# A one-core hybrid layer and a two-layer GLU/attention stack in fp32: another order of the mixer's steps, a fourth buffer for the split weights, and most weight differences moved from GpSimd to VectorE

## The chip, the core and the metric

One NeuronCore of a Trainium2 chip runs the whole program; the other cores are idle. The metric is device time in microseconds of one execution, as the median of several. In a profile PE is TensorE's matmul, PEld its weight load, DVE VectorE, ACT ScalarE, POOL GpSimd and SP the engine whose queue issues the weight loads. An "L" and a number is a line of the kernel.

## What is computed

Input is one sequence of 256 tokens with 1024 features. A first block (state-space scan, a top-k attention, an attention to a memory, a mixture of 32 experts) is followed by two layers of this form:

```python
for l in range(2):
    h = rmsnorm(x, ffn1_norm[l])
    x = x + 0.5 * swiglu(h, ffn1_w_gate[l], ffn1_w_up[l], ffn1_w_down[l])   # 1024 -> 2816 -> 1024
    h = rmsnorm(x, mix_norm[l])
    q_a, k_a, v_a, q_b, k_b, v_b, r_b, g_lr, gate_a, gate_b = split_cols(h @ w_in[l], IN_SPLITS_2)
    o_a = swa_attention(q_a, k_a, v_a, q_gain, k_gain, sinks, cos, sin)     # 8 heads of 64, window 128
    log_a = log_sigmoid(g_lr @ gla_w_gate[l] + gla_gate_bias[l]) / 16
    o_b = gla_attention(q_b, k_b, v_b, log_a)                              # 4 heads, chunks of 64
    o_b = rmsnorm(o_b, gla_out_norm[l]) * silu(r_b)
    merged = sigmoid(gate_a) * (o_a @ w_proj_a[l]) + sigmoid(gate_b) * (o_b @ w_proj_b[l])
    x = x + merged @ w_out[l]
    h = rmsnorm(x, ffn2_norm[l])
    x = x + 0.5 * swiglu(h, ffn2_w_gate[l], ffn2_w_up[l], ffn2_w_down[l])
```

All of it is fp32. The part between the two GLUs is called the mixer here.

## The kernel before, in words

**Units.** A weight matrix comes as units of 128 partitions x 2048 values (1 MB): four 128-row blocks of 512 columns (a `panel` of 1024 rows is two units, `kh` 0 and 1). In the two layers each unit goes through four stations: SP loads it into one of three buffers `raw`; ScalarE copies it, rounded, into one of three `w_hi` (`hi`, L1682); an engine subtracts, `w_lo = raw - w_hi`, into one of three `w_lo`; TensorE takes three products for each block, hi x hi, lo x hi and hi x lo (`split_products`, L969 to L971), 24 matmuls a unit. SP may load unit n once the difference of unit n-3 is made (semaphore `lo_split`), ScalarE may round unit n once TensorE is done with unit n-3 (`unit_used`). In the GLUs the differences are VectorE's (`lo`, L2177). In the mixer the first two (`qa`) are VectorE's and the other 34 of a layer (`mid[2:]`) are GpSimd's (L3185), which has nothing else to do there.

**The order of the work** is written out by hand on each engine; nothing is scheduled. Between its own steps ScalarE rounds the next units by a helper `ahead`, one or two beyond the step at hand. TensorE takes in a mixer, in this order: panels `qa`, `kva`, `qb`, `kb`, the turned heads (`sqT`, `skT`), `glr`, the decay product `lgT` (L1582), then for each half t of the tokens the scores (L1114), panel `vb` c=t, the turning of the probabilities (L1128) and their product with the values (L1253); then panels `rb` 0 and 1 and `ga` 0, the turned keys `gkT`, `A` (L1604), `kv` (L1615), panels `ga` 1 and `gb` 0, the GLA output `ob` (L1629, L1633), panel `gb` 1, `pa`, the turned rows `o`, `pb`, `wo2` with the turned rows `m2` and `n3` between, and then the GLU `ff2`.

**What the others do meanwhile.** VectorE: squares and norm of the heads, rotation (L2395 to L2412), the score's mask and maximum (L2504 to L2515), the normalising (L2519 to L2523), the decay chain that goes back and forth with ScalarE (L3060 to L3086: a running sum L3065 within chunks, exponents on ScalarE between), the GLA state (L3104), the output rows (L3119), the split of turned activations (`a_lo`, L2195, L2210), the weighting by the gates (L3135 to L3140). ScalarE: `hi`, copies out of PSUM (L1689), the softmax's exponents (L1831), the exponents of the decays, roots and the three gates; `rb` is copied raw and goes through Silu after both panels.

**The scan of the first block.** For 16 tiles T TensorE computes an input `bu` (`drive`, L1198), VectorE rotates and scans it (L2351 to L2364), GpSimd rotates back (L3193 to L3201, two buffers `s_out`), TensorE reads out (`read_out`, L1188, L1190). A `drive` needs one of four PSUM banks. To fill the time TensorE also takes 20 pieces of panels (L1057), one a tile up to T=11 and two a tile from T=12. Before tiles 1, 5 and 9 VectorE computes angles of 8.5 us for ScalarE's sine tables.

**The GLU loops** run four trips of six units as hardware loops on TensorE, ScalarE, VectorE and SP, and then a tail.

Of the kernel before, what the change touches and what calls it, by code (L numbers as in the profile page):

```python
# [47 lines left out]
SPLIT = 3  # L48
# [5 lines left out]
SCAN_PIECES = [(n, kh, t) for n in SCAN_PANELS for kh in range(2) for t in range(2)]  # L54
IN2 = dict(qa=(0, 512), kva=(512, 256), qb=(768, 512), kb=(1280, 512), vb=(1792, 1024),
# [63 lines left out]
def plan():  # L119
# [263 lines left out]
    mark("gates", "rb", "ga", "gb")  # L383
# [6 lines left out]
    small_bank[0] = 0  # L390
    small(("rrow", "n2"))
    for t in range(2):
        small(("sqT", t))
    small(("skT", 0))
    panel("qb")
    fill(("qbT", 0), 4); fill(("qbT", 1), 5)
    panel("kb")
    fill(("kbT", 0), 6); fill(("kbT", 1), 7)
# [4 lines left out]
    for i, n in enumerate(("vb", "rb", "ga", "gb")):
        for c in range(2):
            panel((n, c))
            for t in range(2):
                if (n, c) != ("gb", 1):
                    fill((n, c, t), 4 + 2 * (c % 2) + t)
    attention("swa", 4)
# [7 lines left out]
    for t in range(2):  # L417
        for hp in range(2):
            fill(("ob", t, hp), 4 + 2 * t + hp)
    fill(("gb", 1, 0), 6); fill(("gb", 1, 1), 7)  # L420
# [20 lines left out]
    assert RAW == SPLIT == 3 and all(n % RAW == 0 for n in units.per.values()), units.per  # L441
# [4 lines left out]
def bass_hybrid_moe_then_swa_gla(nc, A, out):  # L446
# [4 lines left out]
    with ExitStack() as ctx:  # L451
# [14 lines left out]
        at_hi, w_hi = placed("w_hi", [P, SPLIT, UNIT], F32R)  # L466
        at_lo, w_lo = placed("w_lo", [P, SPLIT, UNIT], F32R)
        raw_r = view_at("raw_r", [P, RAW, UNIT], at_raw, F32R)
        lo_f = view_at("lo_f", [P, SPLIT, UNIT], at_lo, F32)
# [50 lines left out]
        def area(off, *shape):  # L520
# [7 lines left out]
            if len(shape) == 4:  # L528
# [62 lines left out]
                   + [(lo_f[:, i, :], w_lo[:, i, :]) for i in range(SPLIT)])  # L591
# [3 lines left out]
        moe_hi = [y_flat[1][:, 1024:1024 + UNIT]] + [w_hi[:, (PRE_UNITS + i) % SPLIT, :] for i in (2, 0, 1)]  # L595
# [52 lines left out]
        gab = area(o, 2, 2, 1024); o += 4096  # L648
# [15 lines left out]
        hid2 = area(o + 3072, 2, 512)  # L664

# [31 lines left out]
        class Engine:  # L697
# [159 lines left out]
        def _(sp):  # L857
# [3 lines left out]
            def load(name):  # L861

                if E.regs:
                    sp.wait_ge(lo_split, E.unit_value(name) - (RAW - 1))
                sp.dma_start(E.view(raw, name), unit_source(name, E.regs)).then_inc(weights_loaded[E.slot(name)], 16)

            def load_loop(tag):
                with sp.Fori(0, trips_of(tag)) as i:
# [80 lines left out]
        def _(pe):  # L949
# [13 lines left out]
            def unit(name):  # L963

                pe.wait_ge(lo_split, E.unit_value(name) + 1)
                return E.view(w_hi, name), E.view(w_lo, name)
# [234 lines left out]

            for T in range(3):
                drive(T)
            for T in range(SSM_TILES):
                if T + 3 < SSM_TILES:
                    drive(T + 3)
                for piece in SCAN_PIECES[T + max(0, T - 12):T + 1 + max(0, T - 11)]:
                    scan_piece(*piece)
                if T >= 2:
                    read_out(T - 2)  # L1210
            read_out(SSM_TILES - 2)
# [99 lines left out]
            def down_unit(k, c, slot, acc, meanwhile=None):  # L1311
                hi, lo = unit(("d", k, c))
                for t in range(2):
                    for j in range(unit_shape[("d", k, c)][0]):
                        at = (slice(None), slot, j, slice(t * P, t * P + P))
                        m = split_products(acc[t][c], y_hi[at], y_lo[at], hi[:, j, :], lo[:, j, :], False, False,
# [5 lines left out]
            def glu_finish(tag, acc, src, w, following):  # L1322
# [11 lines left out]
                down_unit(k, 0, 0, acc, turn_end)  # L1334
                pe.wait_ge(done["hidden_turned"], nth("hidden_turned", (*z, 1)))
                down_unit(z, 0, 1, acc)
                for t in range(2):
                    close((tag, "acc", 0, t), acc[t][0])
                down_unit(k, 1, 0, acc, following)
                down_unit(z, 1, 1, acc)  # L1340
# [1961 lines left out]
```

## Time and profile before

| | before |
|---|---|
| median of 3 runs | 2443.76 us (2443.68 to 2447.91) |
| profiled execution | 2445.01 us, its span 2443.2 us |
| granted TensorE clock, mean | 0.969 |
| busy: PE / DVE / ACT / POOL | 2290.7 / 1500.2 / 1156.2 / 403.9 us |
| chain that ended last | PE 72%, DVE 15%, ACT 6%, issue 4%, POOL 2% |
| HBM read | 494.45 MB, 203 GB/s over the span |

The span is the time from the first to the last instruction of the profiled execution; 1.8 us of that execution's time lie outside it. Stages by time: first block without experts 0 to 412 us, experts to 1100, then layer 0 with its mixer from 1292.8 to 1589.4, and layer 1 with its mixer from 1962.4 to 2257.6. The mean clock is that of TensorE as granted, 1.00 for 2.4 GHz; the lower level is 1.2 GHz.

### The profile page before, as it was taken

Reading aid. Unit: us, or ns where it says so; the run is one execution under the profiler, and the core shown is the slowest. Engines: PE = TensorE matmul, PEld = TensorE weight load, DVE = VectorE, ACT = ScalarE, POOL = GpSimd, SP = SyncE. Lnnn points to the kernel's source line nnn. Section 1 sums busy time; section 2 is a strip of 40 time slices with the busy share of each in tenths; the row PEclk is TensorE's granted clock in tenths of the full one; section 3 lists DMA queues with packets and bytes.
Section 4 is the critical chain, followed back from the end, with each engine's and each line's share of the span. In section 5 each row is a group of like instructions: output and inputs, shape, how many; then the busy total and the mean of one; then the engine's idle time right before and its main releaser. Section 6 shows DMA issues by size and latency. Waiting matters only on the chain.

```text
span 2443.2 us, 27659 instructions
## 1 busy us (share of the span) xinstructions
PE 2290.7 (94%) x9901; PEld 1637.4 (67%) x9901; DVE 1500.2 (61%) x1497; ACT 1156.2 (47%) x1174; POOL 403.9 (17%) x147
## 2 busy tenths in 40 slices
PE   6899995999999999999999888999999998899999
PEld 4345544566565656548888766788888887667887
DVE  6967337888888887875556442555554573435554
ACT  4122413676767666645334545443343345464432
POOL 2640000000000000000005355600000043555000
PEclk8899997999999999999999889999999999999999
DMA  6234242899999999974545243455455452434553
GB/s 218 69 104 137 87 159 96 329 367 356 373 357 369 358 370 360 368 308 161 183 155 166 78 138 106 154 189 189 163 197 179 156 165 73 134 121 155 189 189 104
DMA packets 166435, 496.64 MB, mean 203 GB/s; under 512 B 10272, under 2 KB 21792, under 8 KB 136400
## 3 DMA queue, kind: packets, MB, share of 16 engines
q1 hardware_dynamic: 164528, 491.70, 57.0%
q10 hardware_dynamic: 1616, 3.24, 0.4%
q8 instruction: 53, 0.87, 0.1%
q0 software_dynamic: 208, 0.59, 0.1%
q14 instruction: 30, 0.25, 0.0%
HBM read 494.45 MB, written 1.05 MB: 203 GB/s over the span
## 4 chain that ended last, share of the span: by engine, by line
PE 72%; DVE 15%; ACT 6%; issue 4%; POOL 2%; DMA 0%; DVEq 0%; ACTq 0%; POOLq 0%
PE ps L969 12%; PE ps L970 12%; PE ps L971 12%; PE ps L1401 9%; PE ps L1037 6%; PE ps L1382 5%; PE ps L1386 5%; PE ps L1128 2%; POOL w_lo L3185 2%; PE ps L1057 2%; PE ps L1370 1%; ACT w_hi L1682 1%; PE ps L1439 1%; PE ps L1253 1%; PE ps L1114 1%
## 5 line engine op out<-in xcount | busy, mean ns | idle before, releaser
L1682 ACT ACTIVATE w_hi<-raw 128x2048 fp32r<-128x2048 f32 x204 | 379.4, 1866 | 423.5 <-PE ps L971 388.7
L3185 POOL TENSOR_TENSOR w_lo<-raw,w_hi 128x2048 fp32r<-128x2048 f32 x68 | 314.6, 4645 | 1558.2 <-ACT w_hi L1682 1558.2
L969 PE MATMUL ps<-w_hi,a_hi 128*128 128x512 f32 (+1 forms) x1216 | 476.0, 391 | 34.2 <-POOL w_lo L3185 23.8
L970 PE MATMUL ps<-w_lo,a_hi 128*128 128x512 f32 (+1 forms) x1216 | 466.3, 383 | 0.0
L971 PE MATMUL ps<-w_hi,a_lo 128*128 128x512 f32 (+1 forms) x1216 | 465.1, 382 | 0.0
L2177 DVE TENSOR_TENSOR w_lo<-raw,w_hi 128x2048 fp32r<-128x2048 f32 (+1 forms) x136 | 303.0, 2229 | 249.0 <-ACT w_hi L1682 243.4
L969 PEld LDWEIGHTS ps<-w_hi,a_hi 128*128 128x128 f32 x1216 | 234.6, 193 | 81.6 <-issue 26.6
L971 PEld LDWEIGHTS ps<-w_hi,a_lo 128*128 128x128 f32 x1216 | 234.2, 193 | 44.5
L970 PEld LDWEIGHTS ps<-w_lo,a_hi 128*128 128x128 f32 x1216 | 234.7, 193 | 40.5
L1382 PE MATMUL ps<-w_hi,W_r 128*128 128x512 f32 x468 | 190.8, 408 | 5.4 <-DVE w_lo L2839 4.7
L969 PE MATMUL ps<-w_hi,y_hi 128*128 128x512 f32 x384 | 153.8, 401 | 0.0
L970 PE MATMUL ps<-w_lo,y_hi 128*128 128x512 f32 x384 | 150.3, 391 | 0.0
L971 PE MATMUL ps<-w_hi,y_lo 128*128 128x512 f32 x384 | 149.8, 390 | 0.0
L1382 PEld LDWEIGHTS ps<-w_hi,W_r 128*128 128x128 f32 x468 | 89.3, 191 | 55.1 <-issue 30.9
L2839 DVE TENSOR_TENSOR w_lo<-lo_f,w_hi 128x2048 fp32r<-128x2048 f32 x48 | 109.2, 2290 | 19.7 <-ACT w_hi L1880 15.8
L1910 ACT ACTIVATE xn<-ps 64x512 f32<-64x512 f32 x78 | 46.4, 595 | 140.8 <-PE ps L1386 139.9
L2839 DVE TENSOR_TENSOR raw_r<-raw,w_hi 128x2048 fp32r<-128x2048 f32 x40 | 90.8, 2290 | 22.5 <-ACT w_hi L1880 20.5
L1401 PE MATMUL ps<-lo_f,W 128*64 128x512 f32 x232 | 103.2, 594 | 0.0
L1401 PE MATMUL ps<-raw,W 128*64 128x512 f32 x216 | 96.5, 596 | 0.0
L1386 PE MATMUL ps<-raw_r,W_r 128*128 128x512 f32 x240 | 95.1, 396 | 0.0
L1386 PE MATMUL ps<-w_lo,W_r 128*128 128x512 f32 x232 | 92.7, 400 | 0.0
L1880 ACT ACTIVATE w_hi<-lo_f 128x2048 fp32r<-128x2048 f32 x48 | 90.4, 1901 | 3.9 <-ACT W_r L1926 2.1
(412 smaller groups left out, 3664.6 us busy)
## 6 DMA issues: line engine op xcount, KB each, us to landing
raw<-in_w_in SPq DMA_DIRECT2D x56, 1024.0 KB, 5.1
raw<-in_ffn_w_gate SPq DMA_DIRECT2D x44, 1024.0 KB, 5.1
raw<-in_ffn_w_up SPq DMA_DIRECT2D x44, 1024.0 KB, 5.1
raw<-in_ffn_w_down SPq DMA_DIRECT2D x40, 1024.0 KB, 5.0
raw<-in_w_up SPq DMA_DIRECT2D x30, 1024.0 KB, 7.9
raw<-in_w_gate SPq DMA_DIRECT2D x30, 1024.0 KB, 7.1
lo_f<-in_w_up SPq DMA_DIRECT2D x30, 1024.0 KB, 8.4
lo_f<-in_w_down SPq DMA_DIRECT2D x29, 1024.0 KB, 7.6
```

The costliest lines, as they stand in the source:

```text
L969: pe.matmul(dst, a_h, b_h, start=first, stop=False, **kw)
L970: pe.matmul(dst, a_h, b_l, start=False, stop=False, **kw)
L971: return pe.matmul(dst, a_l, b_h, start=False, stop=final, **kw)
L1037: m = pe.matmul(dst[t][:, 0:w], lhs[:, k0 + k, t * P:t * P + P], b[:, k, :], start=i == k == 0, stop=i == last and k == nk - 1 and t == 0, ...
L1382: m = pe.matmul(dst, a, hi[:, k * 512:k * 512 + 512], start=half == 0 and k == 0, stop=False, skip_group_check=True)
L1386: m = pe.matmul(dst, a, lo[:, k * 512:k * 512 + 512], start=False, stop=half == 1 and k == 3, skip_group_check=True)
L1401: m = pe.matmul(dst[c], hidT[:, 2 * half + r, :], w[:, r * D + c * 512:r * D + c * 512 + 512], start=half == 0 and r == 0, stop=half == 1 ...
L1682: act.activation(E.view(w_hi, name), E.view(raw, name), ACT.Copy).then_inc(hi_split, 1)
L1880: act.activation(E.expert_hi(u), E.expert_raw(u)[0], ACT.Copy).then_inc(expert_hi, 1)
L2177: tt(E.view(w_lo, name), E.view(raw, name), E.view(w_hi, name).bitcast(F32), ALU.subtract)\
L2839: tt(E.expert_raw(u)[1], E.expert_raw(u)[0], E.expert_hi(u).bitcast(F32), ALU.subtract).then_inc(expert_lo, 1)
L3185: pool.tensor_tensor(E.view(w_lo, name), E.view(raw, name), E.view(w_hi, name).bitcast(F32), ALU.subtract)\
```

## The change

- **Buffers.** Four `hi` and four `lo` buffers (`SPLIT = 4`); the fourth pair lies in the back of `y_hi` and `y_lo`. `raw` stays at three. The end rows of the GLU's hidden values, which lay there, go to a part of W.
- **Differences.** In a mixer VectorE makes 30 of the 36 (28 more than before), GpSimd six: the two of `gb` 1 and the four of `rb`.
- **Order.** `ga` and `gb` come before `rb`; the two units of a panel are steps of their own on TensorE (`wide(n, c, kh)`), with the attention's steps put between units. Scores of both halves come early, and the second half's probabilities lie in the area of the gates, so that they don't wait for the first half's. `rb` leaves PSUM through Silu, the single large Silu is gone. `o` is turned half by half between `pa` and `pb`.
- **Scan.** Four of the pieces go to the tiles before which VectorE computes angles (two after T=1, one after T=5 and T=9); from T=12 there is one a tile. ScalarE copies the panels' results out before it computes tables 2 and 3.
- **Loops.** The GLU loops of the two layers are written out, on all four engines.

```diff
-SPLIT = 3
+SPLIT = 4
+PIECES_WAITING = {1: 2, 5: 1, 9: 1}
...
+        hi_bufs, lo_bufs = ([w[:, i, :] for i in range(RAW)] + [y[:, 1024:1024 + UNIT]]
+                            for w, y in ((w_hi, y_flat[0]), (w_lo, y_flat[1])))
...
-                with pe.Fori(0, trips_of(tag)) as i:
+                for i in range(trips_of(tag)):
...
+            pieces = list(SCAN_PIECES)
             for T in range(SSM_TILES):
                 if T + 3 < SSM_TILES:
                     drive(T + 3)
-                for piece in SCAN_PIECES[T + max(0, T - 12):T + 1 + max(0, T - 11)]:
-                    scan_piece(*piece)
+                scan_piece(*pieces.pop(0))
                 if T >= 2:
                     read_out(T - 2)
+                for _ in range(PIECES_WAITING.get(T, 0)):
+                    scan_piece(*pieces.pop(0))
...
+                scores(0)
+                wide("vb", 0, 0)
...
+                wide("vb", 0, 1)
+                scores(1)
+                wide("vb", 1, 0)
+                turn_probs(0)
+                wide("vb", 1, 1)
                 pe.wait_ge(done["values"], nth("values", "swa"))
...
+                attended(0)
+                wide("ga", 0, 0)
+                turn_probs(1)
+                wide("ga", 0, 1)
+                attended(1)
+                wide("ga", 1, 0)
+                wide("ga", 1, 1)
+                wide("gb", 0, 0)
+                wide("gb", 0, 1)
                 pe.wait_ge(done["decayed"], nth("decayed", "ku"))
...
-                pool.wait_ge(lo_split, E.unit_value(("kva", 0)))
-                for name in mid[2:]:
-                    lo(name)
+                pool.wait_ge(lo_split, E.unit_value((("gb", 1), 0)))
+                for name in straight((("gb", 1), 0), (("rb", 1), 1)):
+                    pool.wait_ge(hi_split, E.unit_value(name) + 1)
+                    pool.tensor_tensor(E.lo_view(name), E.raw_view(name), E.hi_view(name).bitcast(F32), ALU.subtract)\
+                        .then_inc(lo_split, 1)
```

The two tables of order below show where the terms of the prediction lie.

TensorE at the start of the scan, before and then with the change. The matmuls into `m_full` are pieces (four for each), those from `W` 128x256 are drives, those from `s_out` read-outs.

```order
L1057 MATMUL ps<-lo_f,m_full 128x512 x4
L1198 MATMUL ps<-W 128x256 x2
L1057 MATMUL ps<-lo_f,m_full 128x512 x4
L1198 MATMUL ps<-W 128x256 x2
L1057 MATMUL ps<-lo_f,m_full 128x512 x4
L1188 MATMUL ps<-s_out,W 32x256
```

```order
L1080 MATMUL ps<-lo_f,m_full 128x512 x4
L1221 MATMUL ps<-W 128x256 x2
L1080 MATMUL ps<-lo_f,m_full 128x512 x12
L998 MATMUL ps<-zero_b 1x1
L1221 MATMUL ps<-W 128x256 x2
L1080 MATMUL ps<-lo_f,m_full 128x512 x4
```

Two further pieces stand ahead of the third drive.

VectorE in the decay chain of a mixer, before and then with the change. `w_lo<-raw,w_hi` and `y_lo<-raw,y_hi` of 128x2048 are differences of units; the CAST and the difference behind it take the second half of the attention's output out of PSUM.

```order
L3060 SCALAR_TENSOR_TENSOR W<-W,xn 128x1024
L3062 TENSOR_SCALAR W<-W 128x1024
L3065 SCALAR_TENSOR_TENSOR xn<-W 128x256 x4
L3069 TENSOR_TENSOR W<-xn 128x1024
L3072 TENSOR_TENSOR xn<-W 128x1024
L3076 SCALAR_TENSOR_TENSOR W<-W 128x1024
L3078 TENSOR_TENSOR W<-xn 128x1024
L3081 SCALAR_TENSOR_TENSOR W<-W 128x1024
```

```order
L3205 SCALAR_TENSOR_TENSOR W<-W,xn 128x1024
L3207 TENSOR_SCALAR W<-W 128x1024
L3210 SCALAR_TENSOR_TENSOR xn<-W 128x256 x4
L3214 TENSOR_TENSOR W<-xn 128x1024
L2267 TENSOR_TENSOR w_lo<-raw,w_hi 128x2048
L2273 CAST y_hi<-ps 128x4x128
L2275 TENSOR_TENSOR y_lo<-ps,y_hi 128x4x128
L3219 TENSOR_TENSOR xn<-W 128x1024
L3223 SCALAR_TENSOR_TENSOR W<-W 128x1024
L3225 TENSOR_TENSOR W<-xn 128x1024
L2267 TENSOR_TENSOR w_lo<-raw,w_hi 128x2048
L3229 SCALAR_TENSOR_TENSOR W<-W 128x1024
```

A difference now stands in VectorE's queue after each return to ScalarE, and the chain starts before the attention's output is out.

## Rows read from the trace of the kernel before

**Rows 1.** The page: the span in 40 equal slices, PE busy and granted clock, in tenths.

```profile
PE   6899995999999999999999888999999998899999
...
PEclk8899997999999999999999889999999999999999
```

**Rows 2.** Busy time by stretch: two mixers, scan, two GLU stretches; columns in the first line.

```profile
core 0: us, PE busy (x) PEld busy (x) DVE busy (x) ACT busy (x) POOL busy (x), PEclk, DMA share, GB/s
...
1292.80:1589.40 296.60, 263.65 (x1308) 213.85 (x1306) 140.10 (x132) 148.32 (x180) 157.90 (x34) 0.94 0.38 126
1962.40:2257.60 295.20, 262.30 (x1309) 212.57 (x1308) 140.32 (x132) 148.32 (x180) 156.69 (x34) 0.94 0.38 127
...
1110.00:1290.00 180.00, 180.00 (x874) 148.41 (x873) 96.25 (x70) 71.44 (x50) 0.00 (x0) 1.00 0.55 181
```

**Rows 3.** Waits of PE in the first mixer (us in total, times, longest), four of ten.

```profile
PE ps L969 <- POOL w_lo L3185: 12.2, 6, 3.8
PE ps L1128 <- DVE W L3140: 4.3, 1, 4.3
PE ps L969 <- DVE a_lo L2195: 3.9, 2, 3.6
PE ps L1098 <- POOL w_lo L3185: 2.5, 1, 2.5
```

**Rows 4.** Chain of the first mixer's decays, a stretch of it: start, us, what.

```profile
1429.05 1.93 ACT w_hi L1682
1431.05 4.97 POOL w_lo L3185
```

**Rows 5.** The same unit of 24 matmuls at two clocks: stretches with their busy times.

```profile
1425.50:1432.70 7.20, 7.12 (x25) 5.52 (x25) 4.78 (x4) 4.04 (x3) 1.68 (x2) 0.78 0.44 146
1468.20:1474.00 5.80, 5.72 (x25) 4.38 (x24) 0.00 (x0) 4.41 (x3) 2.96 (x1) 1.00 0.00 0
```

**Rows 6.** Timeline of DVE, two places of the first mixer: start, us.

```profile
1319.19 1.23 DVE L2395 TENSOR_TENSOR W<-W,C 128x1024 f32<-128x1024 f32 x1 [3.32 <-ACT C L1698]
1320.45 5.54 DVE L2398 TENSOR_TENSOR W<-W,C 128x1024 f32<-128x1024 f32 x1
...
1549.67 0.69 DVE L3138 TENSOR_TENSOR W<-ps,W 128x512 f32<-128x512 f32 x1
1550.40 4.16 DVE L3140 TENSOR_TENSOR W<-W 128x512 f32<-128x512 f32 x1
```

**Rows 7.** DVE's groups in the first mixer: busy us, mean ns, idle before.

```profile
L3140 DVE TENSOR_TENSOR W<-W 128x512 f32<-128x512 f32 x4 | 15.2, 3812 | 0.1
L2195 DVE TENSOR_TENSOR a_lo<-W,a_hi 128x512 fp32r<-128x512 f32 x10 | 13.3, 1328 | 1.2 <-ACT a_hi L1720 0.3
```

**Rows 8.** The difference on DVE (page) and POOL's (its tile, ns min/median/max).

```profile
L2177 DVE TENSOR_TENSOR w_lo<-raw,w_hi 128x2048 fp32r<-128x2048 f32 (+1 forms) x136 | 303.0, 2229 | 249.0 <-ACT w_hi L1682 243.4
...
L3185 POOL TENSOR_TENSOR w_lo<-raw,w_hi x34: 1447/4606/5672, 1300.7 to 1575.7; 128x2048 fp32r<-128x2048 f32 x33, 128x128 fp32r<-128x128 f32 x1
```

**Rows 9.** The page: loads of units, count, KB each, us from issue to landing.

```profile
raw<-in_w_in SPq DMA_DIRECT2D x56, 1024.0 KB, 5.1
```

**Rows 10.** The scan: PE's waits, then the last rows of DVE and POOL.

```profile
PE ps L1198 <- DVE xn L2353: 18.9, 3, 8.7
...
152.65 1.57 DVE L2364 TENSOR_TENSOR_SCAN W<-W,xn 128x256 f32<-128x256 f32 x1
...
158.74 1.30 POOL L3193 TENSOR_TENSOR xn<-W 128x512 f32<-128x512 f32 x1
160.12 1.26 POOL L3195 TENSOR_TENSOR W<-W 128x512 f32<-128x512 f32 x1
165.19 0.73 POOL L3199 TENSOR_TENSOR s_out<-W,xn 128x256 f32<-128x256 f32 x1 [3.81 <-PE ps L1190]
166.00 0.73 POOL L3201 TENSOR_TENSOR s_out<-W,xn 128x256 f32<-128x256 f32 x1
```

**Rows 11.** Waits of DVE in the first mixer: us in total, times, longest.

```profile
DVE C L2519 <- ACT xn L1831: 10.8, 2, 5.4
```

More of the change, by code:

```diff
@@ L382, in plan @@
     mark("evacuated", *(("ob", t, hp) for t in range(2) for hp in range(2)))
-    mark("gates", "rb", "ga", "gb")
+    mark("evacuated", *(("rb", c, t) for c in range(2) for t in range(2)))
+    mark("gates", "ga", "gb")
+    for t in range(2):
+        mark("maxed", ("swa", t)); mark("exped", ("swa", t)); mark("probs", ("swa", t))
+        mark("probs_turned", *(("swa", t, p) for p in range(4)))
+        mark("branch", ("swa", t))
     panel("qa")
@@ L394, in plan @@
     small(("skT", 0))
[L395 to L398, printed above, removed]
     unit(("glr", 0), 8, 16)
     small(("glrT", 0))
+    for p in range(4):
+        small(("swa", "S", 0, p))
     for i in range(2):
         small(("lgT", i))
[L403 to L409, printed above, removed]
+    for n, c in ((n, c) for n in ("vb", "ga", "gb", "rb") for c in range(2)):
+        panel((n, c))
+        for t in range(2):
+            fill((n, c, t), 4 + 2 * c + t)
+    for p in range(4):
+        small(("swa", "S", 1, p))
+    for t in range(2):
+        for p in range(4):
+            small(("swa", "PT", t, p))
+        small(("swa", "O", t))
     for t in range(2):
@@ L418, in plan @@
         for hp in range(2):
[L419 to L420 removed]
+            small(("ob", t, hp))
     mark("rstd", "o")
@@ L439, in plan @@
     end(LAYERS)
-    assert RAW == SPLIT == 3 and all(n % RAW == 0 for n in units.per.values()), units.per
+    assert RAW == 3 and all(n % RAW == 0 for n in units.per.values()), units.per
     assert tiles.per["moe"] % MOE_RAW == 0 and tiles.n == 6 * TILES
@@ L1539, in glu @@
                 acc = zeroed_sums(tag)
-                with pe.Fori(0, trips_of(tag)) as i:
+                for i in range(trips_of(tag)):
                     regs[tag] = i
@@ L1721, in turned_hi @@
                         act.wait_ge(done["turned_hi"], nth("turned_hi", (tag, hh, t)))
-            def ahead(name, extra=1):
-                split_ahead(E, stretch, hi, name, extra)
             act.wait_ge(const_loaded, 16)
@@ L2001, in glu @@
                 silu((tag, "first"), dst, 512, None, r)
-                with act.Fori(0, trips_of(tag)) as i:
+                for i in range(trips_of(tag)):
                     regs[tag] = i
@@ L2176, in lo @@
                 dve.wait_ge(hi_split, E.unit_value(name) + 1 + ahead)
[L2177 removed]
+                tt(E.lo_view(name, ahead), E.raw_view(name, ahead), E.hi_view(name, ahead).bitcast(F32), ALU.subtract)\
                     .then_inc(lo_split, 1)
[L2180 to L2181 removed]
             def split_out(src, hi_, lo_):
@@ L2958, in glu @@
                 dve.wait_ge(done["rstd"], nth("rstd", root))
-                with dve.Fori(0, trips_of(tag)) as i:
+                for i in range(trips_of(tag)):
                     regs[tag] = i
-                    step.begin(i, steps)
                     lo(("g", L, 0))
```

380 lines of the change are left out of this document (253 added, 127 removed).

## The prediction

> **What bounds the kernel now.** The page's rows by slices of 61 us come first [rows 1]: TensorE is under 90% busy in eight slices of 40, and the five of them behind the first block (numbers 22 to 24 and 33 and 34, from 0) lie in the two mixers, 1292.8 to 1589.4 us and 1962.4 to 2257.6; in the first of them the clock is down too. The table of busy time by stretch [rows 2] says how much is there. In the first mixer TensorE is busy 263.65 of 296.60 us at a clock of 0.94, in the second 262.30 of 295.20 at 0.94; in a GLU stretch of 180 us it is busy 180.00 at 1.00, so that there is nothing to win in the GLUs. Idle are 32.95 and 32.90 us. What the clock costs is read from one pair [rows 5]: the same unit of 24 matmuls takes 7.2 us after a wait of TensorE and 5.8 us in a stretch without one. A clock of 0.94 over a mixer is at most 0.06 x 296.6 = 17.8 us, and 17.7; a part of it lies in the waits themselves and costs nothing more, so I take 15.5 each, that is eleven units at 1.4. TensorE's own work in a mixer is then 263.6 - 15.5 = 248 us.
>
> Who holds it up is in the waits [rows 3]: the differences of GpSimd 12.2 + 2.5, VectorE behind three other steps. The chain [rows 4] shows why a unit comes late: ScalarE rounds it (1.93), and only then GpSimd takes 4.97, all of it seen by TensorE, because the rounding stood behind the chain of decays.
>
> The timeline of VectorE [rows 6] shows a second cost of GpSimd's work. Two operations of 128x1024 follow each other, the first takes 1.23 us and the second 5.54; a 128x512 that reads PSUM takes 0.69 and the next, with both inputs in SBUF, 4.16. In groups [rows 7]: L3140 has 15.2 us for four where 0.69 each would be 2.8, and L2195 has 13.3 for ten where it would be 6.9. That is 12.4 + 6.4; with the same subtraction for the other lines of this kind I count some 45 us of 140.1 in a mixer in which VectorE stood behind GpSimd.
>
> **The change part by part.**
>
> *28 differences from GpSimd to VectorE.* The difference takes 2.23 us in the mean there, with its smaller forms, and 4.6 us on GpSimd [rows 8]. A full one is 2.29, so VectorE gets 28 x 2.29 = 64 us and loses the 45 us of blocking, but for what the last six units leave of it: 140 + 64 - 45 = 159 us of 248, or 64%. ScalarE stays at 148.3 [rows 2]. Neither is full; TensorE is the bound if the units are ready in time.
>
> *Are they?* I laid the three queues beside each other by the durations of these rows, from the first `qa` unit on as time 0. TensorE takes a unit in about 5.6 us; a load lands in 5.1 [rows 9] and rounding takes 1.9 [rows 4]. With four buffers ScalarE may round three units ahead. The narrow places are these, as the time at which the thing is ready and the time at which TensorE wants it: the turned heads' source 39 and 42 (10 us of VectorE after the roots, where the blocked ones take 23 now); probabilities of the first half 67 and 71; the turned probabilities 75 and 78; `ga` 0 78 and 82; decays `k` 116 and 122; GLA state 140 and 144; output rows 170 and 177; `m2` first half 200 and 201; `m2` second half 211 and 210.6; its `a_lo` 214 and 213. All the other units are ready 7 us or more ahead. So nine places are met with 1 to 7 us to spare and the last two are not. I leave 8 us for each mixer: 5.5 of idle time, which is the two late ones and half of what nine places with a mean slack of 4 us can miss, and 2.5 for two units at the lower clock. The bounds are 0 (all are met) and 24 (each of ten places misses by 1 us and pays 1.4 us for a slow unit behind it). **Term: -(48.4 - 8) = -40.4 us for each mixer, -80.8 for both**, between -65 and -97.
>
> *The six that stay with GpSimd.* They are rounded from about 108 to 142 and wanted from 124 to 166, one each 5.6 us or slower because of `kv` and `ob` between. At 4.6 us each they keep up, by 11 us or more. VectorE has then only the last decays (one or two blocked, 3 to 4 us each, with 6 us to spare) and operations that read PSUM. The trace says what the other direction costs: among GpSimd's 34 differences beside a busy VectorE the longest is 5.67 against a median of 4.61 [rows 8], so 1.1 us more at most. The Trainium skill (SBUF — State Buffer, Who interferes with whom) says that a VectorE instruction with two SBUF inputs and a GpSimd one that reads SBUF exclude each other for the whole instruction, whichever came first. By it each of the six could stand 2.3 us behind a difference on VectorE, 14 us in all and not 6.6; the slack of 11 us at the first unit would not be used up at once, so the sum would be the same, but the third rival gets more weight from it. VectorE's part of the rule the trace bears out [rows 6].
>
> *Order of the softmax, Silu by panels, `o` by halves.* The work is the same. Their gain is inside the term above: the waits for VectorE's L2523, L3055, L2187 and for `a_lo` [rows 3] go under units.
>
> *Scan.* TensorE waits three times for a bank, 18.9 us together [rows 10]; four pieces of some 3.6 us, 14.4 us, go there and are missing behind T=12. What that is worth is set by the others: VectorE's last scan ends at 152.65 + 1.57 = 154.2, and nothing TensorE does differently makes it earlier by more than 0.7. GpSimd turns that tile only after a wait of 3.81 us for TensorE's read-out, and is done at 166.7; unhindered its four steps of 1.30, 1.26, 0.73 and 0.73 with gaps end at 154.2 + 4.3 = 158.5. **Term: -8.2 us**, between 0 (ScalarE's later tables hold up the copies out of PSUM, and the pieces with them) and -14.4. Behind the scan TensorE is busy with gates, so this is kept.
>
> *Loops written out.* TensorE is busy 180.00 of 180.00 us over a loop with its trips [rows 2]; a trip's end costs nothing that could be saved. Zero, with all queues of TensorE's six units a trip as cover. The Trainium skill (Runtime: NRT & Kernel Launch, Instruction fetch mechanics) states that a taken branch out of the loaded window forces a fetch, and that kernels prefer unrolling. By it the loops' ends would give something back; no row shows it.
>
> *Buffers, end rows.* No instruction more. The fourth pair is free in the GLUs because the end rows moved. Zero.
>
> **Sum.** 2445.0 - 80.8 - 8.2 = 2356.0 for the profiled execution. That one stands 1.25 us above the median of the runs, 2443.8, so I say **2354.8 us**, 3.6% faster. A measurement of this kernel tells 0.2%, 4.9 us, from no change.
>
> **Rivals.**
>
> 1. *Half of the mixers' loss stays.* VectorE's queue is in order, and its differences now stand behind its own waits for ScalarE; a unit that misses makes `raw` free later, then load, rounding and difference (5.1 + 1.9 + 2.3 = 9.3 us) follow, of which only 5.6 lie under the unit before. For it: the narrow places above. Against it: `raw` of the next units is loaded well ahead in my three queues. It gives 2445 - 48.4 - 8.2 = 2388, median 2387.
>
> 2. *Slower: VectorE's waits become TensorE's.* VectorE waits in a mixer some ten times for ScalarE or for a bank between two differences; the softmax's wait is 5.4 us now [rows 11]. If each reached TensorE in full, with a slow unit behind it, that is 10 x (5.4 + 1.4) = 68 us in a mixer against 48.4 today: 2 x 19.6 - 8.2 = 31 us slower, 2476. It decides from (96.8 + 8.2) / 20 - 1.4 = 3.9 us a place. Against it: three units are rounded and split ahead, 17 us of TensorE's work.
>
> 3. *GpSimd's six hold up `rb`.* With `rb` now last, a late difference there is followed by `pa`, whose difference VectorE makes only after GpSimd's last. Six times (2.3 + 1.4) less the slack of 11: 11 us in a mixer, 2377.
>
> 4. *The change does not do what it says*, because the mixers wait for the weights: then TensorE's idle time stays as it is and only the scan is gained, 2437. Against it: the DMA engines have a share of 0.38 in a mixer, and 0.55 in the GLUs, where TensorE never waits [rows 2].
>
> **How the numbers follow.** My forecast 0.75, rival 1 0.12, rival 3 0.06, rival 4 0.02, rival 2 0.03, and 0.02 for no change by several small things. The forecast's own range is 2445 - 97 - 14.4 = 2334, less 1.25 = 2332, to 2445 - 65 - 0 = 2380; its ends meet only if all terms go one way, so I take 2338. At the top the range goes to 2382, which takes in rival 3. Faster by over 0.2%: 0.75 + 0.12 + 0.06 + 0.02 = 0.95; within: 0.02; slower: 0.03.
>
> **What would show it.** Mixers of 256 us (first `qa` unit to the GLU) with TensorE idle under 8 us and a clock of 0.98 or more in each; all slices from 1100 us on at 9 in both rows of the page; the rotation's and the gates' operations on VectorE (now L2398, L3140) at 1.2 and 0.7 us; VectorE busy some 160 us in a mixer and GpSimd some 28; the last read-out of the scan at 159 to 160 us. The forecast is wrong if TensorE's waits for a difference come back under VectorE's name with more than 8 us, if VectorE is over 80% busy in a mixer, if TensorE's units in a mixer stay at 7.2 us, or if a GLU stretch is below full.

## The result, and the profile after

| | before | after |
| --- | --- | --- |
| time, median | 2443.72 us | **2349.31 us** (2348.77 to 2350.29, 4 runs) |
| ratio of after to before | | 0.9612, 95% interval 0.9595 to 0.9629 |
| profiled execution: its time, its span | 2445.0, 2443.2 us | 2350.29, 2348.2 us |
| mixer 1, first `qa` unit to the GLU | 296.6 us | 251.0 us |
| mixer 2 | 295.2 us | 247.7 us |
| last read-out of the scan | 167.8 us | 160.0 us |

The change makes the kernel 3.9% faster; the prediction was 2354.8 us in a range of 2338 to 2382. The page of the changed kernel, its slices and its counters; it answers to [rows 1]:

```profile
PE 2260.8 (96%) x9901; PEld 1615.0 (69%) x9901; DVE 1536.2 (65%) x1553; ACT 1150.2 (49%) x1172; POOL 144.8 (6%) x91
...
PE   7889996999999999999999999999999999999998
...
PEclk9989997999999999999999999999999999999999
```

From the eighth slice on every digit of both rows is a 9, but for the last of the upper row, where five of these were below it in the upper row before. What the mixers hold now, in the busy time by stretch (columns in the first line; mixer 1, mixer 2, a GLU stretch), answers to [rows 2]:

```profile
core 0: us, PE busy (x) PEld busy (x) DVE busy (x) ACT busy (x) POOL busy (x), PEclk, DMA share, GB/s
1290.30:1541.30 251.00, 248.12 (x1309) 202.77 (x1308) 158.29 (x160) 146.65 (x179) 27.48 (x6) 0.99 0.44 149
1914.70:2162.40 247.70, 244.87 (x1307) 200.64 (x1306) 158.25 (x160) 146.59 (x179) 27.49 (x6) 1.00 0.45 151
1100.00:1280.00 180.00, 180.00 (x873) 148.53 (x872) 96.77 (x70) 74.63 (x55) 0.00 (x0) 1.00 0.51 170
```

TensorE is idle 2.9 us in each mixer where it was 32.9. All but 0.1 us of it stands in two rows of its waits in mixer 1 (us in total, times, longest), and mixer 2 has the same two; the ten of before [rows 3] are gone:

```profile
PE ps L1137 <- DVE W L3149: 2.3, 1, 2.3
PE ps L1121 <- issue: 0.5, 1, 0.5
```

VectorE is blocked at one place only. Its timeline at the rotation, which had 1.23 and 5.54 us [rows 6], and its groups in mixer 1, where the gates' weighting (now L3292) had 3812 ns and `a_lo` (now L2283) 1328 ns [rows 7]:

```profile
1319.19 1.22 DVE L2483 TENSOR_TENSOR W<-W,C 128x1024 f32<-128x1024 f32 x1
1320.44 1.23 DVE L2486 TENSOR_TENSOR W<-W,C 128x1024 f32<-128x1024 f32 x1
```

```profile
L2283 DVE TENSOR_TENSOR a_lo<-W,a_hi 128x512 fp32r<-128x512 f32 x10 | 6.9, 692 | 0.8
L3231 DVE TENSOR_TENSOR W<-xn 128x1024 f32<-128x1024 f32 x1 | 5.5, 5507 | 0.0
...
L3292 DVE TENSOR_TENSOR W<-W 128x512 f32<-128x512 f32 x4 | 2.8, 693 | 0.1
```

That place is one operation of the decays, L3231, which one of GpSimd's six units holds up: 5.5 us where its neighbours of the same size take 1.2. The six themselves (GpSimd's line, both mixers, ns min/median/max) show no slowing; before, the longest took 5672 ns [rows 8]:

```profile
L3375 POOL TENSOR_TENSOR w_lo<-raw,w_hi x9: 4552/4583/4674, 1415.6 to 2059.7; 128x2048 fp32r<-128x2048 f32 x9
L3375 POOL TENSOR_TENSOR y_lo<-raw,y_hi x3: 4604/4608/4662, 1405.3 to 2041.3; 128x2048 fp32r<-128x2048 f32 x3
```

The scan is another matter. PE's timeline at its end answers to [rows 10]:

```profile
153.19 0.62 PE L1211 MATMUL ps<-s_out,W 128*32 128x256 f32 x2 [1.67 <-POOL s_out L3360]
...
158.09 1.06 PE L1211 MATMUL ps<-s_out,W 128*32 128x256 f32 x2 [3.85 <-POOL s_out L3360]
158.94 1.06 PE L1213 MATMUL ps<-s_out,W 128*32 128x256 f32 x2
159.79 0.24 PE L998 MATMUL ps<-zero_b 128*1 128x1 bf16 x2
159.96 16.03 PE L1060 MATMUL ps<-raw,a_full 128*128 128x512 f32 x32
...
183.24 14.00 PE L1060 MATMUL ps<-lo_f,a_full 128*128 128x512 f32 x32
```

The last read-out ends at 160.0, 7.8 us earlier than the 167.8 of before. But TensorE has nothing left to do while it waits 1.67 and 3.85 us for GpSimd, and what follows runs slower: a read-out 1.06 us and not 0.62, the first gate 16.03 us where the next, of equal size, takes 14.00. The same work behind the scan, from the start of that first gate to the same scores, in the kernel before and in the changed one, by stretch (columns as above):

```profile
167.80:287.20 119.40, 115.13 (x412) 63.77 (x409) 66.99 (x124) 42.28 (x79) 0.00 (x0) 1.00 0.36 117
```

```profile
159.96:284.46 124.50, 120.22 (x411) 66.04 (x408) 67.00 (x124) 42.31 (x79) 0.00 (x0) 0.96 0.33 110
```

At a clock of 1.00 it took 119.4 us, at 0.96 it takes 124.5. In this one execution only 7.8 - 5.1 = 2.7 us of the scan's gain are left at the end of that stretch. So two questions stand: is that give-back a property of the change, and which part of the change earned the mixers' 93 us?

### The profile page after: what moved, and what is told of

Read it like the earlier page. It is cut to its first block, busy times and chain, and to the rows that moved or that the text cites. A ratio compares the mean times of both kernels' runs of the same rounds, so it can differ in the third digit from the quotient of the medians.

```text
span 2348.2 us, 26777 instructions
## 1 busy us (share of the span) xinstructions
PE 2260.8 (96%) x9901; PEld 1615.0 (69%) x9901; DVE 1536.2 (65%) x1553; ACT 1150.2 (49%) x1172; POOL 144.8 (6%) x91
## 4 chain that ended last, share of the span: by engine, by line
PE 81%; DVE 12%; issue 4%; ACT 3%; POOL 0%; DMA 0%; DVEq 0%; ACTq 0%; POOLq 0%
PE ps L992 15%; PE ps L993 14%; PE ps L994 14%; PE ps L1428 9%; PE ps L1060 7%; PE ps L1409 5%; PE ps L1413 5%; PE ps L1151 3%; PE ps L1397 2%; PE ps L1466 1%; PE ps L1137 1%; DVE W_r L2927 1%; DVE xn L2445 1%; ACT w_hi L1935 1%; DVE W L2450 1%
## 5 line engine op out<-in xcount | busy, mean ns | idle before, releaser
L2267 DVE TENSOR_TENSOR w_lo<-raw,w_hi 128x2048 fp32r<-128x2048 f32 (+2 forms) x144 | 315.6, 2204 | 126.5 <-ACT w_hi L1737 119.9
L1737 ACT ACTIVATE w_hi<-raw 128x2048 fp32r<-128x2048 f32 (+2 forms) x153 | 281.3, 1848 | 212.1 <-PE ps L994 178.3
L992 PE MATMUL ps<-w_hi,a_hi 128*128 128x512 f32 (+1 forms) x904 | 347.8, 385 | 0.0
L993 PE MATMUL ps<-w_lo,a_hi 128*128 128x512 f32 (+1 forms) x904 | 341.5, 378 | 0.0
L994 PE MATMUL ps<-w_hi,a_lo 128*128 128x512 f32 (+1 forms) x904 | 341.1, 377 | 0.0
L2267 DVE TENSOR_TENSOR y_lo<-raw,y_hi 128x2048 fp32r<-128x2048 f32 x48 | 110.0, 2293 | 50.0 <-ACT y_hi L1737 47.6
L1737 ACT ACTIVATE y_hi<-raw 128x2048 fp32r<-128x2048 f32 x51 | 97.8, 1917 | 59.9 <-PE ps L994 50.3
L992 PE MATMUL ps<-y_hi,a_hi 128*128 128x512 f32 (+1 forms) x312 | 120.1, 385 | 1.3 <-DVE a_lo L2283 1.3
L993 PE MATMUL ps<-y_lo,a_hi 128*128 128x512 f32 (+1 forms) x312 | 116.8, 375 | 0.0
L994 PE MATMUL ps<-y_hi,a_lo 128*128 128x512 f32 (+1 forms) x312 | 116.6, 374 | 0.0
```

The source lines that it names most:

```text
L992: pe.matmul(dst, a_h, b_h, start=first, stop=False, **kw)
L993: pe.matmul(dst, a_h, b_l, start=False, stop=False, **kw)
L994: return pe.matmul(dst, a_l, b_h, start=False, stop=final, **kw)
L1737: act.activation(E.hi_view(name, ahead), E.raw_view(name, ahead), ACT.Copy).then_inc(hi_split, 1)
L2267: tt(E.lo_view(name, ahead), E.raw_view(name, ahead), E.hi_view(name, ahead).bitcast(F32), ALU.subtract)\
```

## The experiments

Each time is a median beside runs of the kernel before on the same chip. The kernel before took 2445.5 to 2447.7 us on the four chips, so it is the ratios that compare across rows; each is uncertain by 0.001 to 0.002, which is 2 to 4 us:

| kernel | us | ratio to before (95%) |
| --- | --- | --- |
| changed kernel, once more (`c_after`) | 2348.9 | 0.9603 (0.9590 to 0.9616) |
| GpSimd makes the mixers' differences (`m1_pool`) | 2377.5 | 0.9713 (0.9698 to 0.9728) |
| two units rounded ahead, not three (`m3_three`) | 2396.4 | 0.9805 (0.9789 to 0.9821) |
| both of these (`m5_pool_three`) | 2399.2 | 0.9799 (0.9783 to 0.9815) |
| the six units on VectorE too (`m2_nosix`) | 2348.1 | 0.9597 (0.9584 to 0.9610) |
| scan as before (`s1_oldscan`) | 2355.0 | 0.9620 (0.9607 to 0.9633) |
| before with the new scan alone (`s3_scan_only`) | 2437.9 | 0.9969 (0.9958 to 0.9980) |
| one piece of the scan held back (`s2_hold`) | 2347.3 | 0.9599 (0.9586 to 0.9612) |
| before with loops written out (`l1_written_out`) | 2446.0 | 0.9996 (0.9987 to 1.0005) |
| low rank first on VectorE (`m4_glr`) | 2339.5 | 0.9566 (0.9553 to 0.9579) |
| three waits taken away (`b2`) | 2336.2 | 0.9550 (0.9537 to 0.9563) |
| the same, six on VectorE (`b3`) | 2335.9 | 0.9543 (0.9530 to 0.9556) |

### Engine, buffer or order?

The changed kernel with the mixers' differences back on GpSimd, everything else kept:

```diff
 def lo(name, ahead=0):
+    if name in mid[2:]:
+        return
...
-pool.wait_ge(lo_split, E.unit_value((("gb", 1), 0)))
-for name in straight((("gb", 1), 0), (("rb", 1), 1)):
+pool.wait_ge(lo_split, E.unit_value(mid[2]))
+for name in mid[2:]:
```

> The changed kernel, but in both mixers GpSimd takes all differences from the third unit on, as in the kernel before; order, fourth buffer pair, scan and written-out loops stay as changed. It tells who earned the mixers' 45.6 and 47.3 us: the engine, or the order and the buffer. Theory A (the prediction's): the engine. VectorE is again held up by GpSimd (rotation's second operation of 128x1024 5.5 us and not 1.23), and a late unit takes 4.6 us of GpSimd where VectorE takes 2.3: mixers of 280 to 297 us against 251 and 248, time 2410 to 2445. Theory B: the order and the three units ahead cover GpSimd's 4.6 us, which lie under a unit's 5.7 us of TensorE: mixers of 250 to 265 us, time 2350 to 2380, though VectorE's operations are as slow as in A.

2377.5 us: theory B. Mixer 1 by stretch, and the longest of TensorE's waits in it:

```profile
1290.00:1552.60 262.60, 248.83 (x1305) 202.12 (x1304) 155.20 (x132) 146.37 (x179) 158.00 (x34) 0.98 0.44 142
```

```profile
PE ps L1151 <- DVE W L2502: 4.6, 1, 4.6
...
PE ps L992 <- POOL y_lo L3377: 0.5, 1, 0.5
```

VectorE's own work is 158.3 less 29 differences of 2.29, some 92 us, so 63 us of its 155.2 are blocking, more than before. (The 92 us hold the 4.3 us by which L3231 was held up, and the 155.2 hold 4.6 us for the two differences that stay with VectorE; the two nearly cancel.) Yet the mixer takes 263 us and not 297 (the second one 265), and hardly a unit is late any more (0.5 us for a GpSimd difference where it was 14.7 [rows 3]). What TensorE waits for are VectorE's own steps: the rotation comes 4.6 us late. Most of the mixers' gain does not need the new engine.

Next, the buffer. All four pairs stay in place, and ScalarE waits as if there were three:

```diff
-act.wait_ge(unit_used, E.unit_value(name) + (ahead - (SPLIT - 1)))
+act.wait_ge(unit_used, E.unit_value(name) + (ahead - (RAW - 1)))
```

> The changed kernel, but ScalarE rounds only two units ahead as in the kernel before, so that the fourth pair of buffers holds nothing that TensorE is not working on. Theory A (the fourth pair carries the order: the units' slack of 7 us or more shrinks by one unit of 5.6 us): TensorE waits for differences behind the chains of ScalarE, 3 to 8 us in each mixer, 2356 to 2370 us. Theory B (the fourth pair does little, VectorE's 2.3 us a unit is quick enough): 2349 to 2353.

2396.4 us: neither. The direction is A's, the size more than twice what A allows. The edit reaches the GLUs' rounding too, but there TensorE stays busy for 300.00 of 300.00 us; the loss lies in the mixers, 276.6 and 272.0 us. By stretch, then the largest waits of TensorE in mixer 1, and ScalarE's timeline ahead of the 6.1 us one:

```profile
1286.40:1563.00 276.60, 257.33 (x1306) 209.51 (x1305) 158.66 (x160) 145.57 (x179) 27.35 (x6) 0.94 0.41 135
1600.00:1900.00 300.00, 300.00 (x1415) 245.78 (x1414) 163.16 (x117) 119.93 (x85) 0.00 (x0) 1.00 0.55 182
```

```profile
PE ps L992 <- ACT W L1744: 6.1, 1, 6.1
PE ps L1151 <- DVE W L3292: 4.2, 3, 2.6
PE ps L1676 <- ACTq L1747: 3.3, 1, 3.3
PE ps L1137 <- DVE W L3149: 3.3, 1, 3.3
```

```profile
1463.59 1.92 ACT L1737 ACTIVATE w_hi<-raw 128x2048 fp32r<-128x2048 f32 x1 [13.55 <-PE ps L994]
1465.41 1.29 ACT L1744 ACTIVATE xn<-ps 128x512 f32<-128x512 f32 x2
...
1475.77 0.21 ACT L1753 ACTIVATE C<-C 128x8 f32<-128x8 f32 x1
...
1479.23 1.49 ACT L1744 ACTIVATE W<-ps,C 128x512 f32<-128x512 f32 x2
```

This is a mechanism that I had under none of my terms. ScalarE's queue is in order, and the rounding of `pa` 0 stands ahead of the copies of `ob`, the output's statistics and the copies of `rb`. With three pairs it may round only when TensorE has let go of a unit, and waits 13.55 us for that. Behind it the copies and statistics start at 1465 and end at 1476; the copies of `rb`, at 1479, are what TensorE then waits 6.1 us for. With the fourth pair the same rounding waits 3.01 us, and the copies of `ob` start 154 us into the mixer and not 179:

```profile
1441.54 1.91 ACT L1737 ACTIVATE w_hi<-raw 128x2048 fp32r<-128x2048 f32 x1 [3.01 <-PE ps L994]
1443.85 0.60 ACT L1744 ACTIVATE xn<-ps 128x512 f32<-128x512 f32 x1 [0.40 <-PE ps L998]
```

No wait of TensorE in that mixer is for a unit; the work behind the rounding comes late. The fourth pair buys ScalarE's queue its freedom, not the units their slack.

Both parts undone together:

> The changed kernel with both of its parts for the mixers undone together, and only their order kept: GpSimd takes the differences from the third unit on, and ScalarE rounds two units ahead. Each undone alone gave 2377.5 us (engine) and 2396.4 us (buffer) against 2348.9. Theory A (the two losses are of the same kind, a unit that is late, and add up or more): 28.5 + 47.5 = 76 us, 2425 us, or above it. Theory B (they cover one another: while TensorE waits for the rounding, GpSimd's 4.6 us are hidden): 2397 to 2410. Against 2440, the kernel before with the new scan alone (2446.4 - 6.1), it tells what the order alone is worth: 15 us or less by A, 30 to 43 by B.

2399.2 us: theory B. The largest waits of TensorE in mixer 1 are those of the buffer's run, with one for VectorE's copies behind the rotation (L3120) added:

```profile
PE ps L1151 <- DVE W L3120: 7.0, 1, 7.0
PE ps L992 <- ACT W L1744: 6.1, 1, 6.1
PE ps L1676 <- ACTq L1747: 3.3, 1, 3.3
```

One more level was needed, the kernel before with the scan's two edits alone (`PIECES_WAITING`, and `tables` behind `vm` and `kvi`):

> The kernel before with nothing but the new order of the scan's pieces and tables. It gives the level from which the order, the buffer and the engine in the mixers start. Theory A (the scan's gain is independent of the mixers): 6.1 us as in the changed kernel (2355.0 against 2348.9), 2440 to 2442 where the kernel before takes 2446.5 to 2447.5. Theory B (in the kernel before, TensorE's clock falls behind the shorter scan too, at 155 and at 200 us, and takes it back): 2444 to 2447. In the profile the last read-out at 160 us in both.

2437.9 us, a ratio of 0.9969: theory A, if anything a little more. With these the change divides, as the difference of the ratios times 2446 us; each of these prices is uncertain by some 3 to 5 us:

| step | from, to | worth |
| --- | --- | --- |
| scan | 1, 0.9969 | 7.6 us |
| order in the mixers, with loops and end rows | 0.9969, 0.9799 | 41.6 us |
| fourth pair, GpSimd still subtracting | 0.9799, 0.9713 | 21.0 us |
| VectorE subtracts | 0.9713, 0.9603 | 26.9 us |

The last two may be taken the other way round, and then they read differently: with three pairs the engine is worth nothing (0.9799 against 0.9805), and the pair on top of it 49 us. Neither figure alone is "the" value of its part; together they are worth 48 us. The 41.6 us are those of all moves of the order together; no run parts them, so which of them earned it (scores early, gates ahead of `rb`, Silu by panels, `o` by halves) stays open.

### Were the six needed on GpSimd?

```diff
-for name in straight((("gb", 1), 0), (("rb", 1), 1)):
-    pool.wait_ge(hi_split, E.unit_value(name) + 1)
-    pool.tensor_tensor(...)
...
 dve.wait_ge(done["decay"], nth("decay", 2))
+lo((("gb", 1), 0))
...
```

and the other five on VectorE behind the decays, the masks and the states.

> The changed kernel with the six units between decays and the output's statistics on VectorE too; GpSimd makes no difference in the mixers. Theory A (VectorE has room: 10.4 and 17.8 us of waiting in that very stretch): VectorE gets 6 x 2.3 = 14 us more in a mixer and TensorE sees none of it, 2347 to 2351 us against 2349.3. Theory B (the split was needed: VectorE's steps of the decays and of the state come late by up to 14 us): 5 us or more in each mixer, 2359 or more. Theory C (GpSimd's six did hold VectorE up): VectorE's operations on the decays shorten and the time falls by over 2 us.

2348.1 against 2348.9 us: theory A. Mixer 1 by stretch, and the decay operation that was blocked:

```profile
1284.90:1535.90 251.00, 248.13 (x1307) 202.94 (x1308) 167.46 (x166) 146.91 (x179) 0.00 (x0) 0.99 0.44 149
```

```profile
L3235 DVE TENSOR_TENSOR W<-W x2: 1219/1219/1219, 1403.5 to 2027.9; 128x1024 f32<-128x1024 f32 x2
```

VectorE gets 13.7 us of differences and gives back 4.3 at that operation: 167.5 for 158.3. TensorE's waits are the same two. The six cost TensorE nothing on GpSimd, and nothing on VectorE.

### Does the scan's gain last?

First the scan of the kernel before in the changed one, with ScalarE's tables at their old places too:

```diff
-scan_piece(*pieces.pop(0))
-if T >= 2:
-    read_out(T - 2)
-for _ in range(PIECES_WAITING.get(T, 0)):
-    scan_piece(*pieces.pop(0))
+for _ in range(1 + (T >= 12)):
+    scan_piece(*pieces.pop(0))
+if T >= 2:
+    read_out(T - 2)
```

> The changed kernel with the scan of the kernel before: one piece at a time and two from T = 12 on, tables before the first three copies. Theory A (most of the scan's gain is given back through TensorE's clock): the last read-out is at 167 to 168 us and not at 160.0, the gate behind it takes 14.0 us and not 16.03, and the time is 2351 to 2354 (2349.3 + 2.7). Theory B (the scan's 8 us are kept to the end, and the difference of 2.7 us at 258 us has another cause): 2356 to 2359.

2355.0 us, 6.1 above the changed kernel, between the two (by the ratios, 0.9620 against 0.9603, it is 4.2 us, give or take 4.5). Its profile says what A says (read-out at 167.8, gate at 14.00 us, no low clock behind), the median nearly what B says. The changed kernel once more explains it:

> The changed kernel unaltered, once more, on the chip of this call: the value that the other kernels of the call are to be held against, and two more mixers and one more scan in a profile. If a fall of TensorE's clock behind a wait is a matter of the single execution and not of the program, this profile shows it in other places than the first one did: behind the scan (at 155 and at 200 us in the first) and behind the 2.33 us wait for the turned heads (mixer 1 yes, mixer 2 no in the first). Time 2347 to 2351 us.

2348.9 us. The clock behind the scan and in the mixers, 10 and 15 us from the end of the scan (155), the first scores (200) and the heads' scores of each mixer, in its profile:

```profile
1335.00:1350.00 15.00, 14.22 (x50) 10.91 (x51) 10.63 (x12) 2.20 (x4) 0.00 (x0) 0.77 0.55 175
1960.00:1975.00 15.00, 14.84 (x53) 11.32 (x54) 10.16 (x11) 2.10 (x5) 0.00 (x0) 0.77 0.59 195
155.00:165.00 10.00, 7.32 (x15) 3.26 (x16) 4.78 (x8) 2.55 (x3) 2.47 (x3) 0.66 0.07 28
200.00:210.00 10.00, 9.94 (x32) 5.45 (x33) 7.19 (x21) 2.39 (x4) 0.00 (x0) 1.00 0.07 28
```

and in the first profile of the same kernel:

```profile
155.00:165.00 10.00, 6.91 (x13) 3.02 (x14) 4.41 (x7) 2.54 (x3) 2.80 (x4) 0.66 0.00 0
200.00:210.00 10.00, 8.99 (x23) 5.28 (x24) 6.53 (x20) 3.18 (x6) 0.00 (x0) 0.66 0.17 67
1335.00:1350.00 15.00, 12.67 (x57) 9.69 (x55) 14.33 (x16) 4.44 (x4) 0.00 (x0) 0.77 0.54 179
1960.00:1975.00 15.00, 12.67 (x67) 9.81 (x65) 13.88 (x14) 5.00 (x6) 0.00 (x0) 1.00 0.49 162
```

So in one kernel the clock falls behind the same wait in one execution and not in the other: at 200 us only in the first, in mixer 2 only in the second. The clock is at 1.2 instead of 2.4 GHz for some 6.8 us (a mean of 0.66 over 10 us is 6.8 us at half speed, one of 0.77 over 15 is 6.9), which costs 3.3 us in a mixer: mixer 2 took 247.7 us without a fall, mixer 1 251.0 with one. Over all profiles: behind the end of the shortened scan with TensorE waiting it fell in 8 of 8, at 200 us in 6 of 9 where the 1.77 us wait there follows a shortened scan, and in none of the three with the old scan; behind the 2.33 us wait in the mixers in 7 of 10. The scan's gain is therefore 8 us less 2 to 3 behind its end (16.03 for 14.00, and twice 1.06 for 0.6), less 3 to 5 more in the executions in which it falls at 200 us too. The end of the stretch above came 1.6 to 7.6 us earlier than before in these eight profiles: 2.7 us in the first, 6.7 us in the second of the same kernel. The medians give 6.1 and 7.6 us.

If the fall behind the scan comes from TensorE's wait, a piece put into that wait takes it away:

```diff
-PIECES_WAITING = {1: 2, 5: 1, 9: 1}
+PIECES_WAITING = {1: 2, 5: 1}
...
 read_out(SSM_TILES - 2)
+scan_piece(*pieces.pop(0))
 read_out(SSM_TILES - 1)
```

> The changed kernel, but one of the 20 pieces is not run at T = 9: it stands between the last two read-outs, where TensorE waits 3.85 us for GpSimd. Nothing is added or left out. Theory A (the clock fell because TensorE waits at the scan's end): the last read-out stays at 160 to 161 us, the gate behind it takes 14.0 to 14.8 us and not 16.03, the granted clock from 159 to 284 us is 0.98 or more and not 0.95, and the time is 2344 to 2347. Theory B (the clock fell for the waits earlier in the scan, or for the read-outs themselves): gate and clock as they are, 2349 to 2352.

```profile
155.00:165.00 10.00, 9.87 (x29) 4.24 (x28) 5.49 (x9) 4.70 (x9) 2.59 (x3) 1.00 0.32 105
200.00:210.00 10.00, 10.00 (x20) 4.54 (x20) 9.25 (x29) 1.79 (x3) 0.00 (x0) 0.68 0.00 0
```

In the profile theory A holds at the scan's end: the read-out ends at 158.8, the clock is 1.00, the gate takes 14.00 us. It fell at 200 us instead. The two later kernels with this held piece also keep a clock of 1.00 there, so it fell in none of three with the piece, against 8 of 8 without. The five times lie from 2344.1 to 2350.9 us, so the median of 2347.3 alone tells neither theory from the other.

### Loops, and what is left

> The kernel before with nothing but the GLUs' loops written out on all queues. Theory A (the prediction's zero: TensorE is 180.00 of 180.00 us busy over a loop with its trips): within 2 us of the kernel before. Theory B (taken branches cost something): 2 us or more under it. Theory C (more code to be fetched costs something): 2 us or more above it.

2446.0 us, ratio 0.9996: theory A, the loops' ends are worth nothing here.

VectorE's order at the turned heads:

```diff
 columns("qbT", qbT)
+columns("kbT", kbT)
 dve.memset(vpad2[:, :, :, :, :], 0.0)...
-lo((("vb", 0), 1))
-columns("kbT", kbT)
...
+lo((("vb", 0), 1))
 lo((("vb", 1), 0))
```

> The changed kernel, but VectorE takes the columns of kb and of the gates' low rank (L3149) ahead of the difference of the second vb unit; that difference follows. TensorE's scores(0) waits for L3149 2.33 us in each mixer. Theory A (these are the last waits in a mixer, and a fall of the clock follows them in some executions): the wait goes to under 0.6 us in both, no window of the mixers has a clock under 1, and the time falls by 2 x 1.9 = 3.8 us, and by up to 2 x 3.3 more where the clock had fallen: 4 to 9 us under the changed kernel on the same chip. Theory B (another wait takes its place, since the vb unit's difference is late now): 0 to 2 us.

2339.5 us, 9.4 less (9.1 by the ratios): theory A, at the upper end of what it allows. The wait is 0.7 us, a little over the 0.6 of the theory, and the clock fell in neither mixer. The same with the held piece, and the turns of the first block's heads moved between the two units of gate 1:

```diff
-gate(1)
-for t in range(2):
-    pe.wait_ge(done["heads"], nth("heads", "dq"))
...
+gate(1, head_turns)
```

> The changed kernel with three waits of TensorE taken away together: a piece of the scan held back for the last wait, the turned heads of the mixers' VectorE queue first, and the turns of the first block's heads put between the two units of gate 1 (TensorE waits 1.77 us for their copies now, and the clock fell behind that wait at 200 us). If waits and the falls behind them are all that is left: 1.2 + 1.77 + 3.8 us of waits, and 3.3 us for each fall that goes, of which the first profile had three: 2334 to 2342. If the waits are merely shifted: 2346 to 2350.

2336.2 us, all five within 0.6 us. The end of the scan, the first scores and both mixers:

```profile
155.00:165.00 10.00, 9.86 (x28) 4.29 (x27) 5.57 (x9) 4.69 (x9) 2.51 (x3) 1.00 0.33 105
195.00:205.00 10.00, 10.00 (x34) 5.25 (x33) 6.99 (x21) 3.08 (x5) 0.00 (x0) 1.00 0.32 105
...
1282.60:1528.60 246.00, 244.79 (x1306) 200.58 (x1306) 158.22 (x160) 146.57 (x179) 27.48 (x6) 1.00 0.45 152
1902.00:2148.00 246.00, 244.82 (x1307) 200.65 (x1305) 158.33 (x160) 146.50 (x179) 27.48 (x6) 1.00 0.45 152
```

A mixer is 246.0 us now, of which TensorE works 244.8 at full clock: nothing is left there. With the six on VectorE too:

> The version with the three waits taken away (2336.2 us), and the six units between decays and the output's statistics on VectorE too, so that GpSimd does nothing in the mixers. In the changed kernel that made 2348.1 of 2348.9 us. Theory A (no difference that can be told): 2335 to 2337. Theory B (without the six VectorE's steps there are no longer held up by GpSimd, at places that TensorE waits for now): under 2334. Theory C (VectorE's queue is now late somewhere): over 2338.

2335.9 us: theory A. The last two kernels are the fastest, 13 us under the changed one, and can't be told apart. TensorE's longest remaining waits lie in the scan, around the experts and at the very start.

## Why the prediction was right, point by point

**Forecast 2354.8, measured 2349.3 us**; it lies in the range, and the direction had 0.95.

- *Mixers, -40.4 each.* Measured in the profiles: -45.6 and -47.5. The idle term was right, 32.95 us gone but for 2.9. The clock term, 15.5, was too small: TensorE's own work is 244.8 us and not 248 (the two mixers above), so the clock had cost 263.6 - 244.8 = 18.8 us, above the 17.8 that I had called the most it could be: the 0.94 of the row has two digits, and with 0.935 the most would be 19.3. The 11 units at 1.4 us that I had put in its place were not counted anywhere. The 8 us left over became 2.9 of idle time and 3.3 of clock in mixer 1, and 2.9 alone in mixer 2: 51.7 - 6.2 = 45.5, and 50.4 - 2.9 = 47.5.
- *The sum.* Two errors met. The profiled mixers gave 12.3 us more than forecast (93.1 for 80.8), and the scan 5.5 us less in that execution (2.7 for 8.2); that the forecast lies only 5.5 us off is in part luck. The upper end of the range was also worked out wrongly: a loss of 24 us in each mixer leaves 2 x 24.4 = 48.8 us of gain and not 65, so the range should have gone to some 2395 us. The 5.5 us of idle time left in each mixer do not follow from the slacks beside them: the two late places are late by 1.4 us in all, and no row gives the rest. Rival 4 should read 2435.6 and not 2437, by the 1.25 us that the other medians have taken off.
- *The timetable.* Of the nine narrow places and the two late ones none was missed but one that it had as 39 against 42, the turned heads, and there not for the heads but for L3149, which stands behind a difference and a memset in VectorE's queue. I had not laid that one in. `m2` and its `a_lo` made TensorE wait for nothing.
- *VectorE 159 us of 248, ScalarE 148.3, GpSimd some 28.* 158.3, 146.6 and 27.5. The 45 us of blocking are right as a count: 140.1 less the 92 us of own work is 48.
- *What earned it.* Here the working named the wrong step, though the time came out. "28 differences from GpSimd to VectorE" stands first in it, and "Buffers, end rows. [...] Zero" near the end; the sum needs no more, but the runs turn it round. The order, with GpSimd and three pairs, gives 41.6 us (the working has the order's gain inside the same term, without a share); the differences moved without the fourth pair give nothing; the pair and the move together 48. Where I used the pair at all, it was as slack for units; it works by keeping ScalarE's queue from standing 13.55 us at a rounding.
- *Six on GpSimd, "they keep up".* Right, with L3231 as the one blocked operation of the "one or two". The estimate by the Trainium skill (SBUF — State Buffer, Who interferes with whom) let each stand up to 2.3 us behind a difference on VectorE. The changed kernel doesn't test that: the twelve lie between 4552 and 4674 ns, but none of them began while VectorE was at a difference. VectorE's part of the rule, the 5.5 us of L3231 for 1.2, is there again. The kernel before shows GpSimd's part as well: two of its differences that begin at 1319.23, just behind the start of VectorE's L2395 [rows 6], take 11.22 us together, where two take 9.2 elsewhere.
- *Scan, -8.2, "so this is kept".* The read-out came at 160.0 as worked out, 7.8 to 8.5 us earlier in all eight profiles of that scan. That it is kept was wrong by the part that the clock takes behind the waits at its end: 6.1 and 7.6 us remain in the medians of the two comparisons. The reason given, TensorE busy with gates, holds for time and not for speed: I had asked what hides the gain, and not what TensorE does in the 5.5 us of waits that the moved pieces left behind.
- *Loops, 0.* Right, by a run of its own: 0.9996. The Trainium skill (Runtime: NRT & Kernel Launch, Instruction fetch mechanics) puts a stall at a taken branch whose target is outside the loaded window; whether these loops' branches leave it no trace here shows, and with the loops written out the time is the same.
- *Rivals.* The first (half of the loss stays, 2387) is near in its time to the change without its fourth pair, 2396, but not in its mechanism: there no unit came late. The second and the fourth saw nothing in any run. The third had six units of GpSimd hold up `rb`: no wait of TensorE for GpSimd in either mixer, and without the six 0.8 us.

## What to carry to other kernels

Ask of an added buffer which queue it frees, and what stands in that queue behind the instruction that waited for it; here one engine does the rounding and the copies in one order, and the quicker step gave nothing (0.9799 and 0.9805) until the buffer was there. Undo the parts of a change in pairs before giving a price to one of them. And where work is moved out of a wait into an earlier one, look at what the engine then does at the old place: a piece left for the last wait of the scan kept TensorE's clock there in all three profiles that had it.

## What the runs showed of the hardware that I had not expected

TensorE's clock falls or stays behind the very same wait from one execution to the next. The 2.33 us wait in the mixers was followed by a fall in 7 of 10 cases, and each fall cost 3.3 us, some 6.8 us at 1.2 GHz. It makes a single profile a poor witness for a difference of a few us: the stretch behind the scan was 5.1 us longer than before in one profile of the changed kernel and 1.5 us in the other. It fits the scatter in part: five times from 2344.1 to 2350.9 us with such waits left in (`s2_hold`), all within 0.6 us where they were gone (`b2`). But the changed kernel, with the same waits, scattered by only 1.3 us in `c_after`, so the scatter is not shown to come from them alone.
